# Half of an output product moved between the steps of the attention, in a hybrid decoder layer

## The reference

```python
proj = rms_norm(x) @ w_in            # nine groups of 512 columns and 8 forget logits
y_pool = pool_mixer(u_pool)          # trailing means less the token, per-group map
y_lru  = gelu(g_lru) * rglru(x_lru)  # conv, gates, linear scan
y_fox  = softmax(q k^T / 8 + c_t - c_s) v              # c: running sum of log f, per head
y_sb   = (exp(log_sigmoid(z) + rest) masked) v         # rest: log(1-beta) summed to the right
y_cat  = rms_norm per group of (y_pool, y_lru, y_fox, y_sb)
x = x + y_cat @ w_out                # 2048 x 2048
x = x + relu(rms_norm(x) @ w_up)**2 @ w_down           # 8192 wide
```

## Time and profile before

| what | value |
|---|---|
| median of three runs | 2926.86 us |
| runs | 2920.7, 2930.03, 2926.86 us |
| profiled execution, its own time | 2931.64 us |
| its span | 2930.0 us, mean granted clock 0.924 |
| TensorE busy | 2698.4 us (92%) |
| VectorE, ScalarE busy | 1292.7 us (44%), 939.7 us (32%) |
| attention loop | 547.9 to 1100.3 us |
| output product | 1154.8 to 1346 us |

### The profile page before, as it was taken

One profiled execution on the slowest core, in us unless ns is written; L12 is line 12 of the kernel. 1 busy time (PEld: TensorE's weight loads), 2 busy tenths in 40 slices (PEclk: granted clock), 3 DMA queues, 4 the chain that ended last, 5 costly groups with the idle time before them and its releaser, 6 DMA issues.

```text
span 2930.0 us, 44015 instructions
## 1 busy us (share of the span) xinstructions
PE 2698.4 (92%) x16970; PEld 2420.6 (83%) x16970; DVE 1292.7 (44%) x1788; ACT 939.7 (32%) x1611; POOL 189.3 (6%) x321
## 2 busy tenths in 40 slices
PE   5999999588888884997999999999999999999999
PEld 4999999244444443997999999999999999999999
DVE  6244432223322325335355445544554455445545
ACT  5244454122222224223233223332332233223323
POOL 0050000322222220000000000000000000000000
PEclk9999999667767766999999999999999999999999
DMA  4283222777767653222222222222222222222222
GB/s 154 88 65 103 85 99 74 238 242 262 257 231 239 230 172 118 87 87 72 87 87 87 85 89 87 87 87 87 87 87 87 87 87 87 87 87 87 87 87 105
DMA packets 104993, 347.74 MB, mean 119 GB/s; under 512 B 29793, under 2 KB 29794, under 8 KB 79602
## 3 DMA queue, kind: packets, MB, share of 16 engines
q1 hardware_dynamic: 84050, 277.45, 28.8%
q0 software_dynamic: 20768, 67.65, 7.1%
HBM read 335.78 MB, written 9.28 MB: 118 GB/s over the span
## 4 chain that ended last, share of the span: by engine, by line
PE 84%; DVE 9%; issue 3%; ACT 2%; DMA 1%; SPq 1%; ACTq 0%; DVEq 0%
PE bank L390 45%; PE bank L395 22%; PE bank L1563 3%; PE bank L1472 2%; PE bank L1522 2%; PE bank L1498 2%; PE bank L1485 1%; PE bank L1474 1%; PE bank L1471 1%; DVE n_tmp L505 1%; DMA w_raw<-weights 1%; DVE sum_tmp L442 1%; DVE w_lo L381 1%; DVE n_tmp L485 1%; DVE x_act L447 1%
## 5 line engine op out<-in xcount | busy, mean ns | idle before, releaser
L390 PE MATMUL bank<-x_act,w_hi 128*128 128x364 f32 (+1 forms) x5616 | 1229.0, 329 | 26.1 <-DVE sum_tmp L442 11.4
L390 PEld LDWEIGHTS bank<-x_act,w_hi 128*128 128x128 f32 x5616 | 897.0, 189 | 31.2 <-DVE sum_tmp L442 13.2
L395 PE MATMUL bank<-x_act,w_lo 128*128 128x272 f32 x3744 | 757.1, 288 | 11.1 <-DVE x_act L447 11.1
L395 PEld LDWEIGHTS bank<-x_act,w_lo 128*128 128x128 f32 x3744 | 651.9, 189 | 20.4 <-DVE x_act L447 18.8
L390 PE MATMUL bank<-hid,w_hi 128*128 128x364 f32 (+1 forms) x3072 | 644.9, 329 | 5.5 <-DVE sum_tmp L442 3.5
L442 DVE TENSOR_TENSOR sum_tmp<-sum_tmp,bank 128x544 f32<-128x544 f32 x336 | 241.9, 720 | 811.0 <-ACT sum_tmp L436 811.0
L390 PEld LDWEIGHTS bank<-hid,w_hi 128*128 128x128 f32 x3072 | 492.6, 188 | 14.5 <-DVE sum_tmp L442 14.5
L435 ACT ACTIVATE sum_tmp<-bank 128x184 f32<-128x184 f32 x336 | 108.8, 324 | 1150.5 <-PE bank L390 1150.5
L381 DVE TENSOR_TENSOR w_lo<-w_raw,w_hi 128x2048 fp32r<-128x2048 f32 x181 | 414.7, 2291 | 85.4 <-ACT w_hi L377 85.4
L395 PE MATMUL bank<-hid,w_lo 128*128 128x272 f32 x2048 | 378.3, 286 | 0.0
L377 ACT ACTIVATE w_hi<-w_raw 128x2048 fp32r<-128x2048 f32 x181 | 346.6, 1915 | 8.7 <-DMA w_raw<-weights 8.7
(11 more groups left out here) (205 smaller groups left out, 1540.7 us busy)
## 6 DMA issues: line engine op xcount, KB each, us to landing
w_raw<-weights SPq DMA_DIRECT2D x181, 1024.0 KB, 4.9
k_ring<-fox_k SPq DMA_DIRECT2D x128, 256.0 KB, 4.2
v_ring<-fox_v POOLq DMA_DIRECT2D x128, 256.0 KB, 3.7
k_ring<-sb_k SPq DMA_DIRECT2D x128, 256.0 KB, 4.1
v_ring<-sb_v POOLq DMA_DIRECT2D x128, 256.0 KB, 3.8
x_in<-xT SPq DMA_DIRECT2D x4, 1088.0 KB, 9.2
kv_out<-proj SPq DMA_DIRECT2D x4, 1088.0 KB
x_res<-xT SPq DMA_DIRECT2D x4, 1088.0 KB, 12.2
```

The costliest lines, as they stand in the source:

```text
L390: ins = nc.tensor.matmul(bank[:, base + b, 0:n], hi, row[:, t:t + n], start=begin, stop=end)
L395: ins = nc.tensor.matmul(bank[:, base + b, 0:HALF], lo, row[:, t:t + HALF], start=False, stop=False)
```

## The change

The output product is cut in two. Its first half takes the inputs of the pooled and the recurrent group.

- In stage 1, `early_squares`, `early_root` and `early_scale` norm these two groups in place, the matmuls with ones after chunks 30 and 32. TensorE waits there for `y_sq`.
- In stage 2, `early_product(i, part_)` multiplies one half (272 columns) of one output tile in step i, with plain fp32 weights (`w_early`, 512 KB a tile, two buffers `wo`), eight matmuls in bank 7, cut into four parts of two. They stand ahead of the scores, between the two turns, ahead of the first weighing and between the weighings. `early_sum` on VectorE adds the residual half, and SyncE stores the sum to `part` in DRAM; stage 3 loads `x_res` from `part`. SyncE issues five more transfers a unit.
- For space, the value ring has three slots for the four chunks of a unit (`V_SLOTS`), and the table `neg_head` goes; a broadcast column of the identity takes its place, with the running sum negated.
- Bank 7 becomes free: the new rows' scores move to bank 5, the transposes of new probabilities and the combined outputs to bank 6, the statistics to bank 4.
- `scores` does both attentions at once; the stick-breaking one takes the other head of the pair, so that its two products of 64 rows lie on different halves of the partitions. `weigh` follows.
- In TensorE's order `seq_sum` moves ahead of the last part and the second weighing; on VectorE `seq_top` moves to the front of the step.
- The loops of loads on SyncE and GpSimd are written out.
- In stage 3 `NORMY` has two groups; `multiply_pair` makes two output tiles from one chunk, eight strips each, eight chunks in all.

```diff
+V_SLOTS, X_SLOTS = 3, 6
...
-    v_ring = r.take("v_ring", [P, 4, 4, D_GROUP])
+    v_ring = r.take("v_ring", [P, V_SLOTS, 4, D_GROUP])
+    wo = [r.take(f"wo{i}", [P, 2 * GT, P]) for i in range(2)]
...
+    def multiply_pair(pe, c0, n, split=None):
+        pe.wait_ge(w_low, c0 + 1)
+        hi = w_hi[c0 % 2][:].rearrange("p (m k n) -> p m k n", m=2, k=2 * GT)
+        lo = w_lo[c0 % 2][:].rearrange("p (m k n) -> p m k n", m=2, k=2 * GT)
+        for m in range(2):
+            pe.wait_ge(evac, n + m + 1)
+            for k in range(2 * GT):
...
+                ins = products(tile_of(n + m), hi[:, m, k], lo[:, m, k], x_act[:, k], k == 0, k == 2 * GT - 1)
...
-    NORMY = [(GT * g, GT) for g in range(4)]
+    NORMY = [(GT * g, GT) for g in range(2)]
+    EARLY = [Y_POOL, Y_LRU]
+    EARLY_AT = [30, 32]
...
+        for u in range(2 * DEC_BATCH):
+            if u + 1 < 2 * DEC_BATCH:
+                load_keys(u + 1)
+            if u >= 1:
+                store_part(2 * u - 2)
+                store_part(2 * u - 1)
+                if u + 1 < KT:
+                    load_early_weights(u + 1)
+            if u + 1 < KT:
+                load_residual(2 * u + 2)
+                load_residual(2 * u + 3)
...
-                    if j == 0 and not first:
-                        pool.wait_ge(d_av, 8 * b + 4 * x + c - 3)
-                    pool.dma_start(v_ring[:, c, j], cache[bass.ds(page, 1)].rearrange("a p n -> (a p) n")
+                    if j == 0 and n >= V_SLOTS:
+                        pool.wait_ge(d_av, n - V_SLOTS + 1)
+                    pool.dma_start(v_ring[:, n % V_SLOTS, j],
+                                   (fox_v, sb_v)[x][bass.ds(page, 1)].rearrange("a p n -> (a p) n")
                                    ).then_inc(v_loaded[c], 16)
...
+        def early_squares(p):
+            y = proj[:, EARLY[p]]
...
+            own.then(v.tensor_tensor(y_sum[:], y[:, 0], y[:, 0], ALU.mult))
+            for t in range(1, GT):
+                own.then(v.tensor_tensor(y_rs[:], y[:, t], y[:, t], ALU.mult))
+                own.wait()
+                ins = v.tensor_tensor(y_sum[:], y_sum[:], y_rs[:], ALU.add)
...
+        def early_sum(i):
+            x = xh[i % X_SLOTS][:]
+            dve.wait_ge(wo_done, i + 1)
+            dve.wait_ge(xh_loaded[i % X_SLOTS], 16 * (i // X_SLOTS + 1))
+            v.tensor_tensor(x, x, bank[:, 7, 0:HALF], ALU.add).then_inc(xh_summed, 1)
...
+            if c in EARLY_AT:
+                pe.wait_ge(y_sq, EARLY_AT.index(c) + 1)
+                pe.wait_ge(head_rs, c - HEAD_AT + 1)
+                for h in range(2):
+                    ins = mm(spare[:, h], ones, y_sum[:, h * HALF:h * HALF + HALF], start=True, stop=True)
+                ins.then_inc(y_mm, 1)
...
+        def scores(i):
             h, q = divmod(i, 4)
+            n = P * (q + 1)
+            o = [HEAD_DIM * (h % 2), HEAD_DIM * ((h + 1) % 2)]
+            s = [bank[:, x, 0:n] for x in range(2)]
             if i >= 1:
+                pe.wait_ge(f_exp, i)
+            mm(s[0], ident[0:HEADS, h:h + 1].to_broadcast([HEADS, P]), c_prompt[:, 0:n], start=True, stop=False)
+            if i >= 1:
+                pe.wait_ge(s_diff, i)
+            for x in range(2):
+                rows = slice(o[x], o[x] + HEAD_DIM)
+                mm(s[x], proj[rows, (FQ, SQ)[x], h // 2, P * q:P * q + P], proj[rows, (FK, SK)[x], h // 2, 0:n],
+                   start=(x == 1), stop=False)
+            for x in range(2):
+                mm(s[x][:, P * q:n], ident, cc(("fox_mask", "sb_mask")[x], 0, P), start=False, stop=True
+                   ).then_inc((f_score, s_score)[x], 1)
...
+        def early_product(i, part_):
+
+            t, h = divmod(i, 2)
+            if part_ == 0:
+                pe.wait_ge(wo_loaded[t % 2], 16 * (t // 2 + 1))
+                if i >= 1:
+                    pe.wait_ge(xh_summed, i)
+            for k in (2 * part_, 2 * part_ + 1):
+                y = proj[:, EARLY[k // GT], k % GT, HALF * h:HALF * h + HALF]
+                ins = mm(bank[:, 7, 0:HALF], wo[t % 2][:, k], y, start=(k == 0), stop=(k == 2 * GT - 1))
+            if part_ == 3:
+                ins.then_inc(wo_done, 1)
...
             if i < UNITS:
-                scores(i, 0)
-                scores(i, 1)
+                early_product(i, 0)
+                scores(i)
             if i >= 1:
                 turn(i - 1, 0)
+            if i < UNITS:
+                early_product(i, 1)
+            if i >= 1:
                 turn(i - 1, 1)
-                weigh(i - 1, 0)
             if odd:
                 seq_shift(u)
+            if i < UNITS:
+                early_product(i, 2)
+            if i >= 1:
+                weigh(i - 1, 0)
+            if odd and u % 2 == 0:
+                seq_sum(u)
+            if i < UNITS:
+                early_product(i, 3)
             if i >= 1:
                 weigh(i - 1, 1)
```

More of the change, by code:

```diff
@@ L125, in build_step @@
     top = r.take("top", [1, P])
+    r.end += 4096
+    xh = [r.take(f"xh{i}", [P, HALF]) for i in range(X_SLOTS - 1)]
     r = Region(A_RAW, A_PROJ)
@@ L315, in build_step @@
     f_y, s_y = sem("f_y"), sem("s_y")
+    y_sq = sem("y_sq")
+    y_mm = sem("y_mm")
+    y_ln = sem("y_ln")
+    y_root = sem("y_root")
+    y_normed = sem("y_normed")
+    wo_loaded = [sem(f"wo_loaded{i}") for i in range(2)]
+    wo_done = sem("wo_done")
+    xh_loaded = [sem(f"xh_loaded{i}") for i in range(X_SLOTS)]
+    xh_summed = sem("xh_summed")
+    xh_stored = [sem(f"xh_stored{i}") for i in range(X_SLOTS)]
     k_loaded = [sem(f"k_loaded{j}") for j in range(4)]
@@ L417, in multiply_tile @@
                 ins.then_inc(strips, 1)
+    def multiply_pair(pe, c0, n, split=None):
[5 more added lines that the diff above has]
+            for k in range(2 * GT):
+                if split is not None and m == 0:
+                    pe.wait_ge(a_low, split + k + 1)
+                ins = products(tile_of(n + m), hi[:, m, k], lo[:, m, k], x_act[:, k], k == 0, k == 2 * GT - 1)
+                if k % 4 == 3:
+                    ins.then_inc(strips, 1)
     def multiply_down(pe, c0, n, per, slot, i=0, step=0):
@@ L916, in seq_logs @@
             own.then(f(d_l[:, 0:SEQ], bank[:, 4], ACT.Abs))
-            own.then(f(d_l[:, SEQ:], bank[:, 7, 0:NEW], ACT.Abs))
+            own.then(f(d_l[:, SEQ:], bank[:, 5, 0:NEW], ACT.Abs))
             own.wait()
@@ L1141, in head_scale, with early_scale @@
                                    ).then_inc(head_norm, 1)
+        def early_squares(p):
+            y = proj[:, EARLY[p]]
+            if p == 0:
+                dve.wait_ge(spare_read, SPARE["pool", GT - 1] + 1)
+            else:
+                dve.wait_ge(y_normed, GT)
+            dve.wait_ge(lru_y, GT)
+            own.then(v.tensor_tensor(y_sum[:], y[:, 0], y[:, 0], ALU.mult))
[3 more added lines that the diff above has]
+                ins = v.tensor_tensor(y_sum[:], y_sum[:], y_rs[:], ALU.add)
+                if t < GT - 1:
+                    own.then(ins)
+                    own.wait()
+            ins.then_inc(y_sq, 1)
+        def early_scale(p):
+            y = proj[:, EARLY[p]]
+            dve.wait_ge(y_root, p + 1)
+            for t in range(GT):
+                v.scalar_tensor_tensor(out=y[:, t], in0=y[:, t], scalar=pcol("out_g", GT * p + t), in1=y_rs[:],
+                                       op0=ALU.mult, op1=ALU.mult).then_inc(y_normed, 1)
         for c in range(C_OUT):
@@ L1241, in seq_max @@
             own.then(v.tensor_reduce(dstat[:, 0:1], bank[:, 4], AX_X, ALU.max, negate=True))
-            own.then(v.tensor_reduce(dstat[:, 1:2], bank[:, 7, 0:NEW], AX_X, ALU.max, negate=True))
+            own.then(v.tensor_reduce(dstat[:, 1:2], bank[:, 5, 0:NEW], AX_X, ALU.max, negate=True))
             own.wait()
@@ L1313, in _ @@
                 prompt_out(i - 1)
-            if odd and u % 2 == 0:
-                seq_top(u)
             if not odd and u < 16 and u % 2 == 1:
@@ L1401, in small_product @@
                 pe.wait_ge(*((spare_read, n) if use[0] != "head" or use[1] == 0 else (head_rs, use[1])))
+            if use[0] == "head":
+                past = sum(at_ < HEAD_AT + use[1] for at_ in EARLY_AT)
+                if past:
+                    pe.wait_ge(y_ln, past)
             for h in range(2):
@@ L1601, in _ @@
         end_stage(pe, 2)
[L1604 to L1607 removed]
+        norm_pe(pe, NORMY, n2_tmp, K_Y, J_Y)
+        for j in range(KT // 2):
+            multiply_pair(pe, C_OUT + j, T_OUT + 2 * j, split=K_Y if j == 0 else None)
+        norm_pe(pe, NORM2, n2_tmp, K_2, J_2)
         def up(c0, t0, i=0, step=0, split=None):
@@ L1700 @@
     mlp.append(down[FF_CHUNKS - 1])
-    weights = np.concatenate([logits, tiles(heads), tiles(a["w_out"][0])] + mlp)
+    w_out = a["w_out"][0]
+    late = tiles(w_out[2 * D_GROUP:]).reshape(KT // 2, 2, P, CHUNK // 2).transpose(0, 2, 1, 3).reshape(-1, P, CHUNK)
+    weights = np.concatenate([logits, tiles(heads), late] + mlp)
```

173 lines of the change are left out of this document (98 added, 75 removed).

## The result

The changed kernel takes 2975.97 us (median of 4 runs, 2970.7 to 2977.47) beside 2926.22 us before on the same chip: a ratio of 1.0168 [1.0147, 1.0189]. That is inside the range of 2875 to 2978 and on the other side of no change than the forecast of 2908.

A forecast was written before the change was run, and what follows sets the result against it. TensorE was taken as the bound, full in attention at low clock with short gaps and in the output product at high clock. Terms -95.0 - 25.8 + 8.8 + 2.8 + 88.0 = -21.2 gave 2908 us, range 2875 to 2978.

The forecast's parts named there:

- Output product -95.0: Output product stage: each tile has half the strips, so 8 x 11.87 us go, -95.0 us.
- Norms -25.8: Norms ahead of the output product: two groups instead of four, 12.9 us each, -25.8 us.
- Squares +8.8: Projection stage: at two chunks TensorE waits for VectorE's squares before its next chunk, 4.4 us twice, +8.8 us.
- Start of the attention +2.8: First scores: four new transfers of 0.70 us stand in front of the decay transfers on SyncE, +2.8 us.
- The attention +88: Attention stage: even unit +7.6 us, odd unit +3.4, so 11.0 a pair, eight pairs +88 us.
- Value chunks: Value product: with three slots the last chunk lands 8.5 us after the start; product 10.5 us against 6.1 and 7.4.
- the even unit, at full clock throughout: Attention, even unit timed step by step at full clock: with its value product 37.0 us against 29.39, +7.6.
- rival D: Value ring: the three slots cost nothing, product back to 6.8 us, -59 us, 2849 us; chance 0.08.
- the overlap: Attention scores: the two 64-row products run as one, gain between 0 and 2.9 us a pair, taken whole.
- A: Odd unit: clock stays low although quarters run there, 8.8 us a pair, +70, 2978 us; chance 0.25.
- B: Attention scores: the two 64-row products do not overlap, 23 us, 2931 us, no change; chance 0.10.
- C: Value chunks land as late as the latest, 6.5 us, +51 us, 2959 us; chance 0.12.

The follow-up runs named there:

- the four-slot version: Changed kernel, complete, with four value slots instead of three, one buffer of output weights filled in four parts and four residual buffers: 2833.22 us, 0.9695 of the kernel before.

## Why the prediction was wrong

Step by step, its own terms, with the stage boundaries of the two profiled executions:

- **Output product -95.0: right.** 14 tiles take 1386.36 - 1303.02 = 83.3 us by the chain that ended last, 5.95 a tile, 95.3 for sixteen, where sixteen took 190.0 before: -94.7.

```profile
1303.02 1.00 PE bank L409 x6
...
1386.36 1.00 PE bank L409 x6
```

- **Norms -25.8: right.** From the last value product to the output product 54.6 us before, 29.3 now: -25.3. A group still takes 12.85 us, from sum to sum in the timeline:

```profile
1278.56 2.15 PE L551 MATMUL bank<-n_tmp,const 128*128 128x272 f32 x4 [4.21 <-DVE n_tmp L518]
...
1291.41 2.18 PE L551 MATMUL bank<-n_tmp,const 128*128 128x272 f32 x4 [10.70 <-DVE n_tmp L518]
```

- **Squares +8.8: right in size and place.** The projection ends 8.0 us later. The timeline at the first of the two chunks shows the wait, 2.64 us instead of 3.4 or 3.5; the sums take 2.1 us instead of the 0.92 I put in, at half clock after it. So the two parts of the term miss in opposite directions:

```profile
433.47 2.08 PE L1562 MATMUL bank<-y_sum,const 128*128 128x272 f32 x4 [2.64 <-DVE y_sum L1235]
```

- **Start of the attention +2.8:** +3.7, near by luck. The first decay transfer leaves at 543.47, only 0.5 us later after the end of the projection than before: the four new transfers stand in front of it, but the key transfers ahead of them leave 2.2 us quicker. What delays the attention is the landing of the last decay transfer, 6.20 us instead of 3.53.
- **The attention +88: wrong, +153.4.** This decides. The timed pair lasts 88.4 us where the steps gave 78.5. The 9.9 are: value product 13.0 and 12.1 us instead of 10.5 (+4.1); the stretch from the unit's start to its first quarter in the even unit 10.1 instead of 6.5 (+3.6); from the odd unit's first quarter to its product 27.4 instead of 24.4 (+3.0); and -0.8 in the even unit's middle. Eight times 9.9 are 79; the stage is only 65 above the forecast, since the difference was put on a mean pair of 69.05 us while the pair timed before was 1.5 quicker than that mean.

All terms together: -94.7 - 25.3 + 8.0 + 3.7 + 153.4 = +45.1, and the spans differ by 2975.6 - 2930.0 = 45.6.

**The step that failed** is "Value chunks" together with "the even unit, at full clock throughout". Its mechanism held, nearly to the tenth: 1.75 + 3.45 + 3.3 = 8.5 us to the last chunk, measured 1.75 + 3.44 + 3.21 = 8.40 in the odd unit (9.33 in the even one, which begins at half clock). The price did not hold. What follows the wait was put at full clock: 2.0 us to the product's end (measured 3.71), the even unit after it full throughout, and 1.5 us for the odd one. By rival D that made the missing slot worth 59 us. The pair of kernels with three and four slots made it **139.5**, and filling the wait showed 55 us of that to be clock alone. A pair of the four-slot version shows where the rest of the error lies: its products take 4.7 and 6.5 us (900.78 to 905.46, 932.31 to 938.77) where rival D went back to 6.8, and its even unit is at the first quarter after 6.4 us, not 10.1. A row of before could have warned: in the earlier trace rows the sum's product behind 10.71 us of idle time takes 2.18 us, half clock. I used it for the price of a product and not for what an idle TensorE does to the work behind it.

Against this the overlap was sized too small: 23 us forecast, 48 and 55 measured. The terms of a pair were read at full clock (0.84 for 384 columns, 1.07 for 512), while the widest ones run at half clock, 2.0 us each. That makes some 7 us of the difference; in the kernel before the mean clock of the stage also rises from 0.70 to 0.77, and how the rest comes about no run separates. So the doubt that no row showed a full overlap was settled the good way and beyond. The row set against the overlap was misread: 857.29 starts the tenth sequence unit, with head 4, where the products of 8 and of 64 rows both start at partition 0 and so lie in the same row group. Only in the even unit of the earlier trace rows, with head 5, do they lie in different ones, 0.40 us each, and there they share a bank.

The rivals. A's time, 2978, was nearly hit, but not by its mechanism: of the odd unit's eight quarters only one (971.82, 2.15 us) is at half clock, with the scores behind it, 7.1 us at 0.50 in all; the others take 1.08 to 1.18. Of A's terms only that for the last chunks came, 1.4 us forecast and 1.7 measured, and in the idle wait it has a cause of its own; the low clock stands behind that wait in both units. B is ruled out by 2.08 against 3.78 us. C is ruled out: landing has a median of 3.2 us. D is ruled out by the 16 waits. The range reached 2978 only through A.

The attention stage, by its length in four kernels: 552.3 us before, 494.2 with the overlap alone, 565.4 with the moved product and four slots, 705.7 with three. That is -58, +71 and +140, together the 153.4. The stage of the kernel before with the overlap alone:

```profile
545.59:1039.77 494.18, 406.89 (x2312) 194.65 (x2312) 161.96 (x420) 135.52 (x374) 130.51 (x243) 0.77 0.76 258
```

The forecast's +88 was made of -23 for the overlap, +71 for the slot (59, and 1.5 us in each of eight odd units) and so +40 for the quarters and all that goes with them. Two of these three errors, -35 and +31, nearly cancel, which is luck; the slot's, +69, is the miss. Why the quarters cost 71 and not 40 is open. Without seven eighths of their columns and half of their products 38 of the 71 go away, and in the 34 that stay the kept products are busy 64 us, while TensorE is busy only 37 us more than with the overlap alone; VectorE's sums and the changes of order were not taken out by themselves. Moving the first quarter behind the scores gives 34 us back, but whether these are the same is not shown.

## What to carry to other kernels

When a buffer ring loses a slot, price the wait and then the clock behind it: here each us of wait on TensorE cost 0.6 us more in the work after it, and products without use in the gap won that back. Before moving work into another stage, look at what it takes there in memory: the moved product cost that stage 71 us for 120 saved in output product and norms, the slot given up for its buffers 140. When a gain is hidden behind a cost, run the one without the other; the overlap alone (-55) and the slot alone (+124) each moved this kernel more than all edits together (+50).

## What was unexpected of the hardware

- After TensorE had stood idle for 5.3 to 5.9 us, the products that followed ran at 1.2 GHz, and the mean clock of the next 14.9 and 10.1 us was 0.61 and 0.67. With the gap filled it was 1.00 over the next 14.7 us.
- Plain fp32 products of 64 rows and up to 512 columns in different halves of the array, into different banks, ran side by side: 2.08 us for two at half clock, 3.78 in the same half.
- Taking 100 us of busy time of the quarters' products out of the stage made it only 38 us shorter: the granted clock fell from 0.88 to 0.79, and TensorE waited 22 us more.
- An fp32 product of one column is not free: 0.21 us between products of other shapes at full clock, where one with 272 columns takes 0.63.
- Added products can make a kernel quicker: 192 of them, -55 us.
